# Dividing the 1152 columns of a unit into 512, 512 and 128 instead of three times 384, in a one-core encoder step

## What is computed

```python
xn = rms_norm(x, g_mix_pre)
q, k, v, o, ig, fg, glu, xq, gates = jnp.split(xn @ w_in, IN_SPLITS, axis=-1)     # 80 units of 128 columns, and 8 gate columns
y_ml = mlstm(q, k, v, ig, fg, state) ...                                          # branch A
y_cv = silu(layer_norm(causal_dwconv(ga * sigmoid(gb)), ln_g, ln_b))              # branch B
y_xa = mem_attention(xq, mk, mv)                                                  # branch C
mixed = sum(sigmoid(gates[i]) * (y[i] @ w_branch[i]) for i in range(3))           # 24 units
x = x + rms_norm(mixed @ w_out, g_mix_post)
fa, fb = jnp.split(rms_norm(x, g_ffn_pre) @ w_ffn_in, 2, axis=-1)                 # 44 units
x = x + rms_norm((silu(fa) * fb) @ w_ffn_out, g_ffn_post)
```

## Time and profile before

| | |
|---|---|
| median of three runs | 2808.9 us (2807.84 to 2810.91) |
| profiled execution, its device time | 2810.57 us |
| span of the profiled execution, first to last instruction | 2808.8 us |
| PE busy | 2686.7 us, 96% of the span |
| DVE, ACT, POOL busy | 1087.8, 625.3, 650.2 us |
| mean granted TensorE clock | 0.985 of full speed |
| traffic with HBM | 105 GB/s over the span |

### The profile page before, as it was taken

How to read it: one execution, slowest core, us unless ns; L and a number is a source line. 1 busy time by engine, 2 the same in 40 slices (tenths; PEclk the granted TensorE clock), 3 DMA queues, 4 the chain that set the end, 5 groups by cost and what they waited for, 6 DMA issues and landing times.

```text
span 2808.8 us, 37457 instructions
## 1 busy us (share of the span) xinstructions
PE 2686.7 (96%) x15080; PEld 2566.7 (91%) x15080; DVE 1087.8 (39%) x1334; ACT 625.3 (22%) x912; POOL 650.2 (23%) x332
## 2 busy tenths in 40 slices
PE   5899999999999999899998898999999999999998
PEld 5899999999999999898888887988999998989897
DVE  3320199999962222216643342245220211110115
ACT  4331111111113233204521141024211110201021
POOL 5421212222221211221201120140313231404131
PEclk9999999999999999999999999999999999999999
DMA  6422333334252223244565534442202020202013
GB/s 180 144 88 88 106 129 121 110 108 142 91 186 80 96 79 105 98 160 106 135 209 177 175 130 147 163 137 90 75 23 68 29 63 23 68 16 68 13 40 135
DMA packets 286828, 294.96 MB, mean 105 GB/s; under 512 B 11386, under 2 KB 250322, under 8 KB 286704
## 3 DMA queue, kind: packets, MB, share of 16 engines
q1 hardware_dynamic: 271800, 239.91, 27.6%
q10 hardware_dynamic: 14912, 53.48, 4.8%
HBM read 208.27 MB, written 85.55 MB: 105 GB/s over the span
## 4 chain that ended last, share of the span: by engine, by line
PE 49%; issue 39%; POOL 8%; DVE 2%; ACT 1%; DMA 1%; SPq 0%; POOLq 0%; DVEq 0%; ACTq 0%
PE PS L1966 19%; PE PS L261 11%; PE PS L1989 9%; POOL w_lo L253 7%; PE PS L1936 3%; PE PS L1531 1%; PE PS L1550 1%; PE PS L1206 1%; PE PS L1214 1%; PE PS L1172 1%; DVE x_T L536 0%; PE PS L1179 0%; DVE y_T L1369 0%; DMA stage<-in_state_conv 0%; PE PS L1167 0%
## 5 line engine op out<-in xcount | busy, mean ns | idle before, releaser
L261 PE MATMUL PS<-A_hi,w_hi 128*128 128x384 f32 x2496 | 573.4, 336 | 17.3 <-DVE A_lo L935 10.0
L261 PE MATMUL PS<-A_lo,w_hi 128*128 128x384 f32 x2496 | 570.9, 335 | 0.0
L261 PE MATMUL PS<-A_hi,w_lo 128*128 128x384 f32 x2496 | 570.4, 335 | 0.0
L253 POOL TENSOR_TENSOR w_lo<-w_raw,w_hi 128x1024 fp32r<-128x1024 f32 x120 | 306.1, 2554 | 1052.6 <-ACT w_hi L249 1052.6
L261 PEld LDWEIGHTS PS<-A_hi,w_hi 128*128 128x128 f32 x2496 | 446.4, 188 | 20.1 <-issue 17.0
L261 PEld LDWEIGHTS PS<-A_lo,w_hi 128*128 128x128 f32 x2496 | 446.5, 188 | 0.0
L261 PEld LDWEIGHTS PS<-A_hi,w_lo 128*128 128x128 f32 x2496 | 446.2, 188 | 0.0
L890 DVE SCALAR_TENSOR_TENSOR c_out<-ext,taps,c_out 128x1024 f32<-128x1024 f32 x480 | 424.1, 962 | 0.7 <-DVE c_out L890 0.7
L249 ACT CAST w_hi<-w_raw 128x1024 fp32r<-128x1024 f32 x120 | 126.3, 1053 | 1079.2 <-PE PS L261 1071.8
L1966 PE MATMUL PS<-A_hi,w_hi 128*128 128x384 f32 x1056 | 242.5, 334 | 2.8 <-POOL w_lo L1881 2.8
L1966 PE MATMUL PS<-A_lo,w_hi 128*128 128x384 f32 x1056 | 242.3, 334 | 0.0
(11 more groups left out here) (289 smaller groups left out, 2766.3 us busy)
## 6 DMA issues: line engine op xcount, KB each, us to landing
proj_d<-stage ACTq DMA_DIRECT2D x80, 576.0 KB, 2.7
w_raw<-in_w_in SPq DMA_DIRECT2D x80, 512.0 KB, 4.2
w_raw<-in_w_ffn_in SPq DMA_DIRECT2D x44, 512.0 KB, 3.9
w_raw<-in_w_branch SPq DMA_DIRECT2D x24, 512.0 KB, 4.3
w_raw<-in_w_ffn_out SPq DMA_DIRECT2D x22, 512.0 KB, 3.4
glu<-proj_d SPq DMA_DIRECT2D x16, 576.0 KB, 5.9
gate_in<-proj_d SPq DMA_DIRECT2D x16, 576.0 KB, 6.4
part_d<-part_out SPq DMA_DIRECT2D x16, 576.0 KB, 4.7
```

The lines of the kernel that those rows point to most:

```text
L253: nc.gpsimd.tensor_tensor(w_lo[:, s % SPLIT, 0:kt], w_raw[:, s, 0:kt], w_hi[:, s % SPLIT, 0:kt].bitcast(F32), ALU.subtract).then_inc(w_lo_ ...
L261: last = nc.tensor.matmul(out, w[:, k], m(k, c), start=start and k == 0 and n == 0, stop=stop and k == kt - 1 and n == 2)
```

## The change

The columns of a unit are cut at 0, 512, 1024 and 1152 (`CUTS`). The first two parts fill a bank each, and the third takes 128 columns of the third bank, so that a unit's 1152 results lie one after another in PSUM (`wide(b)`, from column 1536 x b), and the instructions that read them have one contiguous run instead of three runs of 384. The number of matmuls and of weight loads is the same. Two kinds of waits follow the new cuts: the first part of the first branch unit needs the layer norm's thirds 0 and 1, and `in_unit` for the first two parts needs 8 tiles instead of 6.

```diff
+CUTS = (0, 512, 1024, NTOK)
...
-        def thirds(t):
-            return t.rearrange("p (c n) -> p c n", c=3)
+        PS_cols = PS[:].rearrange("p b c -> p (b c)")
+
+        def wide(b):
+
+            return PS_cols[:, 1536 * b:1536 * b + NTOK]
...
-                    nc.scalar.activation(thirds(stage[:, s % 2]), PS[:, 3 * (s % 2):3 * (s % 2) + 3, 0:TC], func,
+                    nc.scalar.activation(stage[:, s % 2], wide(s % 2), func,
...
         def a_hi(k, c):
-            return A_hi[:, k, TC * c:TC * (c + 1)]
+            return A_hi[:, k, CUTS[c]:CUTS[c + 1]]
 
         def a_lo(k, c):
-            return A_lo[:, k, TC * c:TC * (c + 1)]
+            return A_lo[:, k, CUTS[c]:CUTS[c + 1]]
 
         def banks(b):
-            return [PS[:, 3 * b + c, 0:TC] for c in range(3)]
+            return [wide(b)[:, CUTS[c]:CUTS[c + 1]] for c in range(3)]
...
                         for c in range(3):
-                            pe.wait_ge((ln_lo, ln_lo_pool, ln_lo)[c], (1, 1, 2)[c])
+                            pe.wait_ge(ln_lo, (1, 2, 2)[c])
+                            if c == 0:
+                                pe.wait_ge(ln_lo_pool, 1)
...
-            def in_unit(u, thirds_, end):
+            def in_unit(u, cuts, end):
                 pe.wait_ge(w_lo_done, IN_JOB[u] + 1)
-                pe.wait_ge(n_lo, 3 * thirds_[-1] + 3)
+                pe.wait_ge(n_lo, CUTS[cuts[-1] + 1] // P)
...
-                        for c in thirds_:
-                            last = nc.tensor.matmul(PS[:, 3 * (u % 2) + c, 0:TC], w_[:, u % 2, k], m_[:, k, TC * c:TC * (c + 1)],
+                        for c in cuts:
+                            last = nc.tensor.matmul(banks(u % 2)[c], w_[:, u % 2, k], m_[:, k, CUTS[c]:CUTS[c + 1]],
...
-                nc.scalar.activation(thirds(vb[:]), PS[:, 0:3, 0:TC], ACT.Tanh, scale=0.5).then_inc(f_th, 1)
+                nc.scalar.activation(vb[:], wide(0), ACT.Tanh, scale=0.5).then_inc(f_th, 1)
```

More of the change, by code:

```diff
@@ L816, in dve_proj @@
             dve.wait_ge(wif_used, 1)
-            steps.mark(nc.vector.tensor_scalar(thirds(g_i[:]), PS[0:H, 3:6, 0:TC], g_bias[0:H, 0:1], None, ALU.add))
-            nc.vector.tensor_scalar(thirds(g_f[:]), PS[32:32 + H, 3:6, 0:TC], g_bias[32:32 + H, 0:1], None, ALU.add).then_inc(gate_read, 1)
+            steps.mark(nc.vector.tensor_scalar(g_i[:], wide(1)[0:H], g_bias[0:H, 0:1], None, ALU.add))
+            nc.vector.tensor_scalar(g_f[:], wide(1)[32:32 + H], g_bias[32:32 + H, 0:1], None, ALU.add).then_inc(gate_read, 1)
             dve.wait_ge(gate_read, 1)
@@ L1027, in body @@
                         dve.wait_ge(part_stored[s % 2], 16 * (2 * lap + s // 2))
-                    nc.vector.scalar_tensor_tensor(out=thirds(part_out[:, s % 2]), in0=thirds(gate_in[:, s % 2]), scalar=1.0,
-                                                   in1=PS[:, 3 * (s % 2):3 * (s % 2) + 3, 0:TC], op0=ALU.add,
+                    nc.vector.scalar_tensor_tensor(out=part_out[:, s % 2], in0=gate_in[:, s % 2], scalar=1.0,
+                                                   in1=wide(s % 2), op0=ALU.add,
                                                    op1=ALU.mult).then_inc(part_mul if n else part_done, 1)
@@ L1039, in merge @@
                 dve.wait_ge(gate_loaded[b], 16 * (J // 2 + 1))
-                nc.vector.scalar_tensor_tensor(out=thirds(gate2[:, b]), in0=thirds(gate2[:, b]), scalar=1.0,
-                                               in1=PS[:, 3 * b:3 * b + 3, 0:TC], op0=ALU.add, op1=ALU.mult).then_inc(part_mul, 1)
+                nc.vector.scalar_tensor_tensor(out=gate2[:, b], in0=gate2[:, b], scalar=1.0,
+                                               in1=wide(b), op0=ALU.add, op1=ALU.mult).then_inc(part_mul, 1)
                 dve.wait_ge(part_mul, J - KT + 1)
@@ L2161, in gate @@
                     dve.wait_ge(f_th, u // 2 + 1)
-                    nc.vector.scalar_tensor_tensor(out=thirds(vb[:]), in0=thirds(vb[:]), scalar=1.0, in1=PS[:, 0:3, 0:TC], op0=ALU.add,
+                    nc.vector.scalar_tensor_tensor(out=vb[:], in0=vb[:], scalar=1.0, in1=wide(0), op0=ALU.add,
                                                    op1=ALU.mult).then_inc(f_v, 1)
@@ L2165, in gate @@
                     dve.wait_ge(f_v, u // 2 + 1)
-                    nc.vector.scalar_tensor_tensor(out=thirds(vb[:]), in0=thirds(vb[:]), scalar=0.5, in1=PS[:, 3:6, 0:TC], op0=ALU.mult,
+                    nc.vector.scalar_tensor_tensor(out=vb[:], in0=vb[:], scalar=0.5, in1=wide(1), op0=ALU.mult,
                                                    op1=ALU.mult).then_inc(f_g, 1)
```

## The result

The changed kernel takes 3029.0 us (median of four, 3028.4 to 3030.3) against 2808.4 us before (the three runs of 2808.9 and one more, beside the changed kernel): a ratio of 1.078, interval 1.077 to 1.080. The forecast was 2995 us, within 2940 to 3040. The profiled execution took 3029.2 us, with a span of 3027.5 us, 218.7 more than before.

What follows compares the result with a forecast made beforehand. The prediction took PE's own matmul pace as the bound. Short-matmul slots 171.3, layer norm wait 6.6, feed-forward wait 5.4 and half clock 2.5 make 185.8 us, added to 2808.9: 2995 us, range 2940 to 3040.

Steps and rivals of the forecast that it cites:

- What bounds the kernel: All units: PE, busy in 96% of the span, sets the time by its own pace; ACT and DVE wait for it.
- A term of zero: ACT's and DVE's reading instructions, one run instead of three: any change is covered by PE's unit of 12.5 us, so 0 us.
- The weight load as the floor under a slot: Units' triples: the next block's load outlasts the short matmul's 66.7 ns, so PE waits for it; 82% chance.
- Its size: Short matmul's slot in the units: 114.6 ns, 47.9 ns over its share, 3576 times, 171.3 us (144 to 204).
- Loads ahead of the two long matmuls have 226.7 ns and stay hidden: 512-column matmuls in the units: they keep their 226.7 ns pace, with nothing added for their weight loads.
- The upper bound of 123.8 ns and 204 us: Short slot at most, from eight 16-column matmuls up to the next matmul's start, 0.99 us / 8: 57.1 ns more.
- The first join: First branch unit: its first matmul waits for layer norm thirds 0 and 1, so the start slips by 6.6 us.
- The half clock after the gap is paid already: First branch unit's restart: the kernel before already runs at half clock there, so no further clock cost.
- The second join: First feed-forward unit: waiting for 8 tiles stops PE for 5.4 us, plus 2.5 us of half clock afterwards.
- The load is hidden anyway: Rival for the units: time is linear in columns, only 14.5 us of waits stay, 2823 us; chance 7%.
- the short matmul runs at the plain float32 rate: Rival for the units: short float32r product takes two records, 223.8 ns, 157.1 ns over its share; 3385 us; chance 8%.
- The short matmul loses its gap: Rival for the units: load hidden, slot of 53.3 ns, each triple 13.3 ns shorter; 2776 us; chance 3%.

## Why the prediction was right, point by point

**What bounds the kernel.** Right. PE's pace was the whole matter: the control with three readers for each unit moved nothing, and ACT's contiguous reader takes 1127 ns where the one over three banks took 1126. "A term of zero" was zero on both sides.

```profile
L681 ACT ACTIVATE stage<-PS 128x1152 f32<-128x1152 f32 x80 | 90.2, 1127 | 0.0
```

**The weight load as the floor under a slot.** Right, and shown by the runs with half of the weights and with half of the columns, and by the load starts: 109 ns beside a short matmul of 64, 128 or 192 columns, 58 ns with half of the weights. The chain of reasoning in the rows (a load's record starts with the matmul ahead, grows with the weight columns, and eight 16-column matmuls keep the pace of 128-column ones) led to the cause before any row of the shape itself existed. The 64-column load's record of 134 ns lies on the line of the earlier trace rows, between 89 and 190.

**Its size.** This is the term that was mis-sized, though it is not the short matmul's own time that fell short. The sum had 114.6 ns for the short one and 2 x 226.7 ns for the long ones ("Loads ahead of the two long matmuls have 226.7 ns and stay hidden"), 567.9 ns in all. The triple took 577.0 ns, and 3576 x 9.1 ns = 32.5 us are nearly all of the 34 us by which the result lies over 2995. Measured by the load starts, the short one occupies 109 ns, which is the prediction's lower estimate (some 108 ns, at 0.84 ns for each weight column), and the long ones take 236 and 232 ns. So the term that was put at nothing is the 15 ns that the two long matmuls lose behind a short one, and 114.6 in place of 109 made up more than a third of it by chance.

The 114.6 was not a pace either: of its seven intervals the first is 133 ns and the other six are 111 to 112. Eight transposes of the kernel before, with 128 weight columns each, have the 109 ns already, though their kind and their load's record (140 ns) are different: 0.87 us / 8.

```profile
1973.64 0.87 PE PS L1946 x8
```

The upper bound of 123.8 ns and 204 us meets the whole loss, but by luck. It holds the interval of 187 ns from the last of the eight to the matmul behind them, whose load does not start with the matmul ahead as the others do, but only here:

```profile
282.98 0.47 PEld L261 LDWEIGHTS PS<-A_hi,w_hi 128*128 128x128 f32 x3
```

That is one pause behind the eight, spread over them, and not a cost of each. Nor did the 256-column pace "rule out" a higher price: 117.3 ns limits the load alone, and the whole price of a short matmul between long ones was 123.7.

**The first join.** Right: 6.7 us for 6.6. "The half clock after the gap is paid already" was right, with about 1 us given back, as the half clock lasted some 3.2 us in place of 5.5. Why it was shorter no run shows.

**The second join.** Right: 5.3 us for 5.4, and 2.3 us for the clock for 2.5. The granted clock fell during this silence of 5.3 us; the window that ends 2.4 us into it still had 1.00.

**The rivals.** "The load is hidden anyway" is thrown out by the run with half of the weights, which has the same number of instructions, and "the short matmul runs at the plain float32 rate" by 111.4 ns in a row. The figure of the Trainium skill for a pair of load and matmul at 128 columns (TensorE: Matmul & The Clock Gate, "Back-to-back issue gap"), 81 ns, is not met either: float32r pairs of that size went at 111.4 ns. "The short matmul loses its gap" was rightly given a small chance, but for an incomplete reason: the gap really is smaller (a slot of 60 ns at most, with half of the weights to load), only the load doesn't let it show.

## What to carry to other kernels

Before cutting a moving operand into unequal parts, read the weight load as a floor: each matmul must last at least as long as the load behind it, here 109 to 111 ns for 128 columns of 4-byte weights. Between long ones the whole price was 120 to 124 ns, so that a part under 256 columns costs as if it had 256. Prefer equal parts over full banks and a rest, and don't add up paces that were measured in runs of equal matmuls; a mixture had 3 to 12 ns of its own for each triple. A contiguous read-out is worth nothing where one instruction over several banks takes as long, and it can cost at the joins, where a wider first part waits for more of its input.

## What the hardware showed that was not expected

- Beside a short matmul the next load starts 109 ns after the one before, whether 64, 128 or 192 columns move, and 58 ns after it with half of the weight columns.
- A short matmul costs more than that: the two 512-column matmuls behind it take 236 and 232 ns, where they take 226.7 among their like. With pairs of short ones some 12 ns come once for a pair (570 ns for a triple instead of 577). The cause stays open.
- A 128-column float32r matmul with half of the weights to load behind it has a slot of 60 ns at most, under 7 over its columns, while 384 and 512 columns have 13.3.
- 256 columns between 384 and 512 take 121 ns and the 512 behind them 234, while between two 448 a slot of 120 in the projection and 127 in the feed-forward layer was measured. The bank column at which the result starts plays no part. What makes the difference was not found.
